# Shift and scale pieces of the modulation laid out with outputs on partitions, summed by one VectorE instruction each

## What is computed

```python
mod = silu(c) @ w_mod[i] + b_mod[i]            # 1024 -> 3072, for each of 4 layers
shift, scale, gate = split(mod, 3)
h = rms_norm(x, norm_pre_g[i]) * (1 + scale) + shift
o = mixer(h)                                   # gla, sgu, fox, gla
x = x + gate * rms_norm(o, norm_post_g[i])
...
top_s, top_i = top_k(s, 16)                    # of 128 keys, on two sides
best_s, pos = top_k(top_s[0][:, None] + top_s[1][None, :], 16)
idx = take(top_i[0][:, None] * 128 + top_i[1][None, :], pos)
gates = softmax(best_s)
y = sum_e gates_e * gelu(x . expert_down[idx_e]) * expert_up[idx_e]
```

## Time and profile before

| what | value |
|---|---|
| runs | 1750.39, 1748.75, 1738.15 us |
| profiled execution | 1739.41 us, span 1737.6 us |
| busy: TensorE, VectorE, ScalarE, GpSimd | 1393.7, 1047.5, 433.1, 490.7 us |
| read from HBM | 589.55 MB, 340 GB/s over the span |
| mean granted TensorE clock | 0.909 |

### The profile page before, as it was taken

The page is one execution under the profiler, slowest core; times in us unless marked ns, Lnnn a source line. Parts: engine busy times, 40 slices in busy tenths (PEclk is TensorE's granted clock), DMA queues, the critical chain, the costliest instruction groups (busy, mean ns, idle before and its releaser), DMA issues. The chain is left out here.

```text
span 1737.6 us, 13867 instructions
## 1 busy us (share of the span) xinstructions
PE 1393.7 (80%) x4158; PEld 717.6 (41%) x4158; DVE 1047.5 (60%) x2197; ACT 433.1 (25%) x974; POOL 490.7 (28%) x498
## 2 busy tenths in 40 slices
PE   6998988978999999999777777699787647666665
PEld 6454435444444455444354343455333312222222
DVE  3645554553233222313797998788866778877876
ACT  1221413423423421102133232132002221111111
POOL 2101210210000000000445546355344545444441
PEclk9998998989999999999897888798888878898898
DMA  9978884978556776887999989999999999999995
GB/s 386 377 256 303 312 340 171 347 282 295 213 207 219 277 265 242 290 293 265 402 361 357 413 339 403 412 400 413 410 414 414 348 412 422 421 422 421 422 421 248
DMA packets 108941, 591.53 MB, mean 340 GB/s; under 512 B 12450, under 2 KB 12706, under 8 KB 60612
## 3 DMA queue, kind: packets, MB, share of 16 engines
q0 software_dynamic: 67776, 312.56, 45.4%
q1 hardware_dynamic: 41092, 278.10, 42.2%
HBM read 589.55 MB, written 1.05 MB: 340 GB/s over the span
## 5 line engine op out<-in xcount | busy, mean ns | idle before, releaser
L948 PE MATMUL bank<-ring,hT 128*128 128x512 f32 x1888 | 866.6, 615 | 39.6 <-DVE room L1920 12.1
L948 PEld LDWEIGHTS bank<-ring,hT 128*128 128x128 f32 x1888 | 366.5, 198 | 482.2 <-issue 449.8
L877 POOL DMA_INDIRECT room<-in_peer_down,idx x92 | 102.5, 1114 | 525.1 <-DVE idx L1781 401.8
L1798 DVE CUSTOM_DVE_ANT_0 room<-room 128x1024 f32<-128x1024 f32 x180 | 218.6, 1221 | 50.6 <-DMA room<-in_pair,idx 38.4
L1203 PE MATMUL bank<-room 128*128 128x512 f32 x284 | 150.9, 676 | 96.5 <-ACT room L1493 94.2
L1813 DVE SCALAR_TENSOR_TENSOR x<-room,pcoef,x 128x1024 f32<-128x1024 f32 x121 | 155.7, 1287 | 28.0 <-DMA room<-in_peer_up,idx 27.5
L877 POOL DMA_INDIRECT room<-in_peer_up,idx x104 | 114.0, 1096 | 88.6 <-DVE pa L1798 42.3
L1203 PEld LDWEIGHTS bank<-room 128*128 128x128 f32 x284 | 57.5, 215 | 190.8 <-issue 97.2
L849 POOL DMA_DIRECT2D room<-in_w_mod x80 | 42.2, 528 | 326.3 <-DVE room L1567 206.5
L877 POOL DMA_INDIRECT room<-in_pair,idx x88 | 97.0, 1102 | 108.5 <-PE bank L1203 50.6
L927 PE MATMUL bank<-cst,room 128*128 128x128 f32 x424 | 64.7, 297 | 55.3 <-ACT room L1439 24.1
(11 more groups left out here) (304 smaller groups left out, 1527.4 us busy)
## 6 DMA issues: line engine op xcount, KB each, us to landing
ring<-in_wpk SPq DMA_DIRECT2D x248, 1024.0 KB, 7.0
room<-in_w_mod POOLq DMA_DIRECT2D x80, 512.0 KB, 8.2
room<-in_w_mod SPq DMA_DIRECT2D x8, 1024.0 KB, 15.8
room<-in_norm_post_g POOLq DMA_DIRECT2D x4, 512.0 KB, 5.0
rowb<-in_gate_bias SPq DMA_DIRECT2D x4, 512.0 KB, 9.0
room<-in_peer_up,idx POOLq DMA_INDIRECT x104, 12.5
room<-in_peer_down,idx POOLq DMA_INDIRECT x92, 12.4
room<-in_pair,idx POOLq DMA_INDIRECT x88, 14.3
```

The source lines that it names most:

```text
L877: return pool.indirect_dma_start(out=dst, out_offset=None, in_=A[table][0] if table != "pair" else A[table], in_offset=bass.IndirectOffset ...
L948: last = mm(bank[p][:, :], lhs, ring[:, h % 4, k * N:(k + 1) * N], start=(kk == 0), stop=(h == halves[-1] and k == 3))
L1798: v.tensor_tensor_reduce(out=row, in0=row, in1=u_(g // MINE), scale=1.0, scalar=0.0, op0=ALU.mult, op1=ALU.add, accum_out=pa[:, g // TOPK ...
```

## The change

1. `w_mod` is packed on the host (`pack_modulation`, outside the timed execution). A shift or scale piece now has its 128 outputs on the partitions and all 1024 inputs along the row; the order of pieces in a layer is shift 0, scale 0, shift 1, scale 1, ..., then the 8 gate pieces as before. Each of the 16 is multiplied with `crow` (`silu(c)` on all partitions) and summed by one `tensor_tensor_reduce`, which gives one finished column of `modr`.
2. `mod_columns` adds the bias from `cst` and makes `modc`, on VectorE alone. The 96 matmul records of L986 and the 128 of L1010 are gone, and `mod_cols` no longer takes a place in the turn of the two banks. All 16 early pieces are on VectorE. SP loads `crow` (512 KB) ahead of them.
3. The pieces 16 to 95 go through six slots instead of four.
4. `choose` has fewer instructions (both sides in one, no casts to float and back).
5. At the query step of tile 0, the first score and the first `choose` stand one product earlier.
6. The last eight picks: their additions come up to four ticks earlier, the last group of four weights is two of two, and of the last four picks TensorE adds 252 and 253, VectorE 254 and 255.

```diff
+def pack_modulation(inputs):
+    pieces = []
+    for w in inputs["w_mod"]:
+        for j in range(KC):
+            pieces += [w[:, third * D + j * P:third * D + (j + 1) * P].T for third in range(2)]
+        pieces += [w[:, 2 * D:].reshape(P, KC, D)[:, k] for k in range(KC)]
+    return np.stack(pieces)
...
-            b(0, name="query", pre=[("norm_in", t, 5)]),
-            b(1, [("score_T", t, 0)], name="query"),
-            b(2, [("score_S", t, 0), ("score_T", t, 1)], name="query"),
+            b(0, [] if t else [("score_T", t, 0)], name="query", pre=[("norm_in", t, 5)]),
+            b(1, [("score_T", t, 0)] if t else [("score_S", t, 0)], name="query"),
+            b(2, ([("score_S", t, 0)] if t else []) + [("score_T", t, 1)], name="query"),
...
-TICKS = PICKS + REST + LEAD[1]
-PIECES = [(L, third, k) for L in range(DEPTH) for third in range(3) for k in range(KC)]
-PE_PIECES = (5, 7, 9, 11, 13, 15)
+TICKS = PICKS + REST + 2
+PIECES = [piece for L in range(DEPTH) for piece in
+          [(L, third, j) for j in range(KC) for third in range(2)] + [(L, 2, k) for k in range(KC)]]
+SLOTS = 6
...
 def added_at(v):
+    if v >= PICKS - 8:
+        return tick_of(PICKS - 2) + (v - PICKS + 8) // 2
     return tick_of(v) + LEAD[v // MINE]
...
-            if name == "query" and n == 2:
+            if name == "query" and n == 1:
                 order.append(("choose", 0))
...
             load(cst[:, 0:CST_FIRST], A["cst"][:, 0:CST_FIRST], "first_in")
+            load(crow, A["c"].to_broadcast([P, D]), "first_in")
...
             def fetch(n):
-                pool.wait_ge(S("summed"), summed_before(2 * KC if n < 2 * KC + 4 else n - 3))
+                pool.wait_ge(S("summed"), max(n - SLOTS + 1, 2 * KC - 4))
...
-                if kind == "mod_cols":
-                    pe.wait_ge(S(f"sums_init{L % 2}"), sums_set(L))
-                    for j in range(2 * KC):
-                        last = mm(bank[p][:, j:j + 1], sums[L % 2][j // KC][:, (j % KC) * P:(j % KC + 1) * P],
-                                  ones[:, 0:1], start=L > 0, stop=True, skip_group_check=L == 0)
...
             def add_piece(n):
+                if third < 2:
+                    v.tensor_tensor_reduce(out=piece, in0=piece, in1=crow, scale=1.0, scalar=0.0, op0=ALU.mult, op1=ALU.add,
+                                           accum_out=modr[:, L, third, k:k + 1]).then_inc(S("summed"), 1)
+                    return
...
+            def mod_columns(L):
+                dve.wait_ge(S("summed"), columns_of(L))
+                link(v.tensor_tensor(modc[:, L, :, :], modr[:, L, :, :],
+                                     const("bmod", 2 * KC * L, 2 * KC).rearrange("p (a b) -> p a b", a=2), ALU.add))
+                v.scalar_tensor_tensor(out=modc[:, L, 1, :], in0=modc[:, L, 1, :], scalar=1.0,
+                                       in1=const("npre", L * KC, KC), op0=ALU.add, op1=ALU.mult).then_inc(S("modc"), 1)
```

More of the change, by code:

```diff
@@ L272 @@
 DVE_NTH = {u: i for i, u in enumerate(ON_DVE)}
-ADDS = {added_at(v): [v] for v in range(PICKS)}
+ADDS = {k: [v for v in range(PICKS) if added_at(v) == k] for k in range(TICKS)}
 def adds_of(k):
-    return ADDS.get(k, [])
+    return ADDS[k]
 def sums_at(hh):
@@ L399, in make_order @@
             pending = []
-            if name == "query" and n == 2:
+            if name == "query" and n == 1:
                 order.append(("choose", 0))
-                rows.tick()
-            if name == "query" and n == 3:
-                rows.tick()
-                rows.tick()
+            if name == "query" and n >= 2:
+                for _ in range(n - 1):
+                    rows.tick()
     order += pending
@@ L479 @@
 for _s in ORDER:
-    if _s[0] in ("mm", "mod_cols", "mod_gate"):
+    if _s[0] in ("mm", "mod_gate"):
         _n = len(USE)
@@ L595, in build @@
         amask = const("amask").rearrange("p (a b) -> p a b", a=4)
-        mring = [at(M0 + i * D, D) for i in range(4)]
+        mring = [at(M0 + i * D, D) for i in (0, 1, 2, 3, 5)] + [at(KTC, D)]
         early = [at(base + i * 2 * D, 2, D) for base, n in ((M0, 2), (AA, 2), (BB, 2), (AA + 5 * D, 1), (BB + 5 * D, 1))
                  for i in range(n)]
+        crow = at(M0 + 4 * D, D)
         gpost = at(M0 + 7 * D, D)
-        sums = [[at(M0 + (4 + i) * D, D) for i in range(3)],
-                [gateb[:, 3, :], at(KTC, D), skT[:, KC:2 * KC, :].rearrange("p a b -> p (a b)")]]
+        gsum = [at(M0 + 6 * D, D), skT[:, KC:2 * KC, :].rearrange("p a b -> p (a b)")]
         def area(t, L):
@@ L854, in start_sums @@
                     pool.wait_ge(S(f"pd{p}"), n // 2 + 1)
[L855 to L858 removed]
+                link(nc.gpsimd.memset(gsum[L % 2], 0.0))
+                pool.dma_start(gsum[L % 2][0:1, :], A["b_mod"][L:L + 1, 2 * D:3 * D]).then_inc(S(f"gsum_init{L % 2}"), 16)
             def fetch_post(L):
@@ L978, in quad_values @@
                 return h_v(t, (n - 4) // 2)[:, head * DH:(head + 1) * DH]
-            def piece_columns(n, p):
-                _, third, k = PIECES[n]
-                pe.wait_ge(S(early_in(n // 2)), 16)
-                for j in range(KC):
-                    mm(bank[p][:, third * KC + j:third * KC + j + 1], early[n // 2][:, n % 2, j * P:(j + 1) * P],
-                       const("cond", k, 1), start=n == PE_PIECES[0] and j == 0, stop=False, skip_group_check=True)
-            pe.wait_ge(S("first_in"), 16)
+            pe.wait_ge(S("first_in"), 32)
             pe.wait_ge(S("ones_set"), 1)
             pe.wait_ge(S("pool_order"), 1)
-            pe.wait_ge(S("cond"), 1)
-            for piece in PE_PIECES[:2]:
-                piece_columns(piece, use("mod_cols", 0)[1])
             for step in ORDER:
@@ L1017, in _ @@
                         pe.wait_ge(S(f"ev{p}"), n // 2)
-                    pe.wait_ge(S("summed"), summed_before((L + 1) * 3 * KC))
-                    mm(bank[p][:, :], ones[:, :], sums[L % 2][2][:, i * N:(i + 1) * N], start=True, stop=True) \
+                    pe.wait_ge(S("summed"), gates_of(L))
+                    mm(bank[p][:, :], ones[:, :], gsum[L % 2][:, i * N:(i + 1) * N], start=True, stop=True) \
                         .then_inc(S(f"pd{p}"), 1)
@@ L1321, in _ @@
                     if s < DEPTH:
-                        evacuated(act, "mod_cols", s)
+                        act.wait_ge(S("modc"), s + 1)
                     for i in range(1 - t, 2):
@@ L1829, in _ @@
                         add_piece(KC + n)
-                    src, done = produced(dve, *step)
-                    v.tensor_copy(modc[:, L, 0, :], src[:, 0:KC])
-                    v.scalar_tensor_tensor(out=modc[:, L, 1, :], in0=src[:, KC:2 * KC], scalar=1.0,
-                                           in1=const("npre", L * KC, KC), op0=ALU.add, op1=ALU.mult).then_inc(done, 1)
+                    mod_columns(L)
                 elif kind == "mod_gate":
```

129 lines of the change are left out of this document (54 added, 75 removed).

## The result

The changed kernel took 1695.41 us (median of 1696.64, 1699.99, 1694.19 and 1690.98), the kernel before 1747.44 us (median of the three runs named at the start and of one more, 1746.13). The profiled execution took 1696.64 us, its span 1694.9 us instead of 1737.6, that is 42.7 us less, where the prediction had 31.4. The direction and most of the places were right, and the gain was larger than forecast.

What follows compares the result with a forecast made beforehand. The first half was taken as bound by TensorE's fixed order, the second by transfers of expert rows. Terms summed to -37.7 us, less 6.3 given back: -31.4, so 1708 us profiled, 1714 median; range 1698 to 1738.

Steps and rivals of the forecast that it cites:

- What bounds the kernel: Whole kernel: a microsecond TensorE saves in the first half moves the second half's start and the end by as much.
- The ends of the layers: Ends of layers 0, 1 and 2: filling products start earlier and run faster; terms -11.0, -7.3 and -6.8 us.
- The gate's sums: Layer 1: with six slots TensorE's wait for L1839 goes and the clock stays up; term -8.6 us.
- The late piece in layer 0: Layer 0, at 84.48: TensorE's wait of 2.49 us behind a late piece goes; term -2.5 us.
- The start: First product ten microseconds earlier, but low waits for posi, which lands later; term +3 us, bounds -6 and +6.
- (a): Rival at the start: the constants are there in time, term -6 instead of +3, 1705 us; chance 0.12.
- VectorE: All 96 pieces on VectorE, a reduction at 1221 ns; six more pieces counted in the start, elsewhere 0.
- Choice and end: Choice of experts: gathers some 7 us earlier, term -3 us; end: fewer additions behind the last weights, -1.5 us.
- The sixth given back: Discount of 6.3 us on the sum: without TensorE's pauses the DMA engines must bring the same bytes in less time.
- (c): Rival: as (b), the start costs +6, choice and end bring nothing; 1738 us; chance 0.10.
- (d): Rival in the weight transfers: six slots starve the weights, with all 13 series 29 us slower; chance 0.04.
- (b): Rival at layer ends and gate's sums: other waits replace half the gains, 16.9 us less, 1731 us; chance 0.27.

Runs made afterwards that it cites:

- e1: The changed kernel with four slots for the pieces instead of six: 1702.21 us, ratio 0.9771 to the kernel before.
- e6: The changed kernel with POOL fetching the last norm_post row behind piece 95 instead of 84: 1695.03 us, ratio 0.9699.
- e10: The changed kernel with e4's and e6's edits, and three pieces of layer 1 moved behind the out1 products: 1687.65 us, ratio 0.9695.
- e11: e10 with no piece behind the very first product (spread 0, 4, 4, 3, 3, 3) and rowb's rows loaded at out0: 1688.52 us, ratio 0.9694.
- e9: The changed kernel once more, unaltered: 1697.69 us, ratio 0.9758.
- e8: The changed kernel with the last eight picks as in the kernel before: 1703.98 us, ratio 0.9757.
- e2: The changed kernel with mod_cols back in the turn of the two banks, with one matmul of one column: 1713.27 us, ratio 0.9838.
- e3: The changed kernel with wlow loaded between the ring halves and low waiting for it instead of all constants: 1696.93 us, ratio 0.9754.
- e4: The changed kernel with POOL asking for the first piece only when the constants have landed: 1691.63 us, ratio 0.9721.
- e7: The changed kernel with first score, first choice and ticks of the query step placed as before: 1706.12 us, ratio 0.9774.
- e12: e11 with the pieces of layer 0 spread 0, 3, 3, 0, 5, 5 over the six products and 5, 5 over out0: 1679.39 us, ratio 0.9631.

## Why the prediction was right, and where it was not

**What bounds the kernel.** Right: what TensorE saved in the first half came off the end one for one, within the scatter of the second half: 37.8 us earlier at 732, 42.7 at the end. In e1, e6, e10 and e11 the last multiplication kept the shift of 732 to within 0.5 us; the largest departures are e9's -3.2 and e8's +5.7.

**The ends of the layers.** Right in place and size: -11.2, -8.0, -5.4 against -11.0, -7.3, -6.8. e2 shows that the bank turn carries the larger part at each of the three (7.3, 4.2 and 7.0 us), and that of the 7.3 in layer 0 the clock behind the pause is 3.0. As forecast, the second filling product did not wait for L1909.

**The gate's sums.** That six slots take away the wait for L1839 was right (e1 brings it back); the size depends on the execution. The step that failed is "the last two transfers are no longer waited for": they are, by the next user of VectorE, L1593. Three more pieces stand there, 3.77 us apart, and TensorE waited 1.7 to 7.5 us behind them. So the term was 2.0 to 9.3 us, not 8.6 for sure, and that e9 comes close to it is luck of the execution. In the first trace 1.7 of the 4.7 have another cause: between 275.5 and 280.7 the kernel before ran five groups of L1080 and L1083 at the lower clock (0.59 granted from 276 to 280, 0.79 to 1.06 us a group instead of 0.59).

**The late piece in layer 0.** Right, -2.5. It is the slots' alone: without them e1 loses 3.0 there.

**The start.** Right: +2.2 against +3, the first product at 36.95 (36 to 39), `posi` at 56.7 (56 to 59). Rival (a) did not come about. Not right was that the product behind it starts at the lower clock: `low` itself paid, 3.56 instead of 1.92 us, with 0.50 granted in the stretch ahead of it, and the product took 7.13. Nor did I see what e3, e4 and e11 show, that the 10 us were not to be had by freeing `low` alone.

**VectorE.** Right at 1220 ns. The Trainium skill's rule in "Vector Engine (DVE) Microarchitecture Reference", section "Points that are easy to get wrong", that two sources in SBUF that are not bf16 halve the rate, is not borne out by this instruction. The page says it of the layout of `scalar_tensor_tensor`, and the prediction had stretched it to the reduction; but `scalar_tensor_tensor` itself, with two such sources, takes 1282 ns here, where a reduction of one source of the same size (L1951) takes 1.21 us. Left out was that reductions follow each other in 1.15 us and additions in 1.31 to 1.38, so that a series of three is at least 0.4 us shorter.

**Layer 2.** The sum had nothing here, and 6.5 and 5.1 us were gained. VectorE in layer 2 of the kernel before, whose rows did not stand ahead of the prediction:

```profile
339.00 3.92 DVE L1567 SCALAR_TENSOR_TENSOR gateb<-room,cst,gateb 128x1024 f32<-128x1024 f32 x3
...
351.70 1.28 DVE L1567 SCALAR_TENSOR_TENSOR gateb<-room,cst,gateb 128x1024 f32<-128x1024 f32 x1 [2.47 <-DMA room<-in_w_mod]
```

```profile
387.30 1.28 DVE L1567 SCALAR_TENSOR_TENSOR room<-room,cst 128x1024 f32<-128x1024 f32 x1 [5.99 <-DMA room<-in_w_mod]
```

I had read TensorE's waits only at the places that the change names, and these late pieces with them not at all. The bank turn accounts for 0.1 of it (e2), and the slots for nothing that can be told: e1 loses 1.4 here, and so does e9 with six slots. The rest could be the shorter series and POOL, which clears one sum instead of three ahead of the pieces; neither was tried, and it stays open.

**Choice and end.** The choice was probably mis-sized: I counted only the free share of the DMA engines, 2 us of 7. The first choice moved by 5.9 us (from 811.26, to 767.53, less the 37.8), and in e7 5.8 us reach the last multiplication. The 3.3 us of the first trace, which look like a hit, and the 6.6 of the second differ by no more than the scatter. The end was right at 1.6; e8 gives up to 3.1.

**The sixth given back.** This step and the missing layer 2 made the forecast too small. No stretch gave anything back that it had gained, and the DMA slices of layers 0 and 1 are at about the same tenths as before. The argument about the ring was one without a row: from 60 to 460 us no pause of TensorE in the timeline of either trace names `ring`, nor is there one that names nobody, as e3's wait for a ring half does. The balance of the first trace is 31.4 + 6.3 (the sixth) + 6.5 (layer 2) + 1.7 (to 732) + 2.1 (start, ends of layers 0 and 1, choice, tail) - 3.9 (gate) - 1.4 (end of layer 2) = 42.7. So that the sum without the discount, -37.7, comes nearer is in part because terms left out and terms too large offset each other.

**Rivals and range.** (a), (c) and (d) did not happen; of (b) only the gate's part, in some executions. The range had its room on the side of a smaller gain, down to (c), and on the other side only rival (a). A gain that was left out had no case there, so the median of 1695 fell just outside of it.

## What to carry to other kernels

A step of no length that takes a turn in a double-buffered bank can cost a whole reading and the clock behind the pause: count the turns, not the instructions. A wait that is taken away from a full queue moves to the next one who stands behind the same transfers: e3 and e4 freed `low` and kept 1.7 and 1.3 of 10 us, and only when the pieces due next had been spread too (e12) did 9.9 stay. An entry in a queue that waits for a late reader holds up everything behind it; asked for last, it cost nothing (e6). And a discount on a sum should have its row, as each of its terms has.

## What was not expected of the hardware

The same program, up to 740 us instruction for instruction the same, waited between 1.67 and 6.81 us at one place in four executions, and the second half came out 3.2 us shorter in one trace and 5.7 us longer in another; the time of a whole run varied by 9 us (1690.98 to 1699.99). At such places a term below 3 us can't be read from one trace. Elsewhere it can: from 75 to 170 us the shifts of e3 to e9 change by less than 0.1. A pause of 3.09 us on TensorE cost another 3.0 us in the product behind it (10.05 instead of 7.03 us for 16 records), about as much as the pause itself; before, the pause of 5.00 us at the same place had cost 2.3 (9.31 instead of 7.03).
